# All low parts behind a norm on VectorE, gate rows split in one piece and placed later, retention's output in two parts

## The reference

```python
def rms_norm(x, w):
    y = xf * lax.rsqrt(jnp.mean(xf * xf, axis=-1, keepdims=True) + EPS)
    return (y * w)
# second block
mod = silu(c) @ w_ada + b_ada                     # shift, scale, gate for three parts
u = rms_norm_2(x, ffn1_norm_g) * (1 + sc1) + sh1
x = x + 0.5 * g1 * swiglu(u, ffn1_w_in, ffn1_w_out)
u = rms_norm_2(x, mix_norm_g) * (1 + sc2) + sh2
z = u @ w_mix + b_mix                             # q, k, v, o, i, f of the mLSTM, q, k, v, f of the attention
# mLSTM: b = cumsum(log_sigmoid(f)); m_t = b + running maximum of (i - b)
# retention, per head: ret = rms_norm(forward + backward); y_ret = silu(rg) * ret
```

## Time and profile before

| | us |
|---|---|
| median of 3 runs | 2095.94 |
| lowest, highest | 2094.49, 2096.2 |
| the profiled execution | 2094.88 |
| its span, first to last instruction | 2093.1 |

### The profile page before, as it was taken

One profiled execution on the slowest core, in us unless ns is written; L12 is line 12 of the kernel. 1 busy time (PEld: TensorE's weight loads), 2 busy tenths in 40 slices (PEclk: granted clock), 3 DMA queues, 4 the chain that ended last, 5 costly groups with the idle time before them and its releaser, 6 DMA issues.

```text
span 2093.1 us, 27478 instructions
## 1 busy us (share of the span) xinstructions
PE 2030.0 (97%) x9476; PEld 1594.0 (76%) x9476; DVE 860.5 (41%) x1237; ACT 773.1 (37%) x1176; POOL 771.0 (37%) x310
## 2 busy tenths in 40 slices
PE   7899999999999999999979999999999999999999
PEld 5677677888888788888857776677788887888887
DVE  5566574342232543442284555444311264222200
ACT  5334343322222322322245555555522243223211
POOL 2222243444443444444323322222244434444443
PEclk9999999999999999999989999999999999999999
DMA  4111134553322455552212221111233222323322
GB/s 147 51 51 41 51 108 164 199 186 95 105 95 81 160 185 196 190 180 97 85 51 61 70 70 51 51 53 57 61 91 100 90 90 80 100 90 100 101 94 95
DMA packets 56641, 210.72 MB, mean 101 GB/s; under 512 B 6288, under 2 KB 7056, under 8 KB 56592
## 3 DMA queue, kind: packets, MB, share of 16 engines
q1 hardware_dynamic: 56592, 210.08, 31.1%
HBM read 207.96 MB, written 2.10 MB: 100 GB/s over the span
## 4 chain that ended last, share of the span: by engine, by line
PE 71%; issue 22%; POOL 5%; ACT 1%; DVE 1%; POOLq 0%; ACTq 0%; DVEq 0%
PE bank L431 62%; POOL wlo L376 4%; PE bank L465 1%; PE bank L714 1%; PE bank L768 1%; PE bank L783 1%; PE bank L794 1%; PE bank L803 1%; POOL xl L387 0%; POOL wlo L381 0%; PE bank L487 0%; PE bank L775 0%; PE bank L772 0%; ACT fraw L1242 0%; DVE sqn L1397 0%
## 5 line engine op out<-in xcount | busy, mean ns | idle before, releaser
L376 POOL TENSOR_TENSOR wlo<-raw,whi 128x1024 fp32r<-128x1024 f32 (+1 forms) x290 | 739.2, 2549 | 1262.5 <-ACT whi L872 1262.5
L431 PE MATMUL bank<-xh,whi 128*128 128x512 f32 x1688 | 685.6, 406 | 39.0 <-DVE xl L1388 13.0
L431 PE MATMUL bank<-xh,wlo 128*128 128x512 f32 x1688 | 662.6, 393 | 0.0
L431 PE MATMUL bank<-xl,whi 128*128 128x512 f32 x1688 | 662.6, 393 | 0.0
L872 ACT ACTIVATE whi<-raw 128x1024 fp32r<-128x1024 f32 (+1 forms) x298 | 330.2, 1108 | 630.1 <-PE bank L431 616.2
L431 PEld LDWEIGHTS bank<-xh,whi 128*128 128x128 f32 x1688 | 319.8, 189 | 120.9 <-issue 33.0
L431 PEld LDWEIGHTS bank<-xl,whi 128*128 128x128 f32 x1688 | 320.3, 190 | 69.8 <-issue 7.7
L431 PEld LDWEIGHTS bank<-xh,wlo 128*128 128x128 f32 x1688 | 319.8, 189 | 68.9
L431 PE MATMUL bank<-acth,whi 128*128 128x512 f32 x528 | 209.0, 396 | 0.5 <-POOL wlo L376 0.5
L431 PE MATMUL bank<-acth,wlo 128*128 128x512 f32 x528 | 208.8, 396 | 0.0
L431 PE MATMUL bank<-actl,whi 128*128 128x512 f32 x528 | 208.8, 395 | 0.0
(11 more groups left out here) (314 smaller groups left out, 2050.3 us busy)
## 6 DMA issues: line engine op xcount, KB each, us to landing
raw<-w_dram SPq DMA_DIRECT2D x250, 512.0 KB, 3.6
adaw<-ada_dram SPq DMA_DIRECT2D x72, 512.0 KB, 4.3
raw<-wd_dram SPq DMA_DIRECT2D x48, 704.0 KB, 4.0
h<-x_dram SPq DMA_DIRECT2D x4, 512.0 KB, 7.4
out_dram<-h SPq DMA_DIRECT2D x8, 256.0 KB, 3.7
rel<-rel_dram SPq DMA_DIRECT2D x1, 513.0 KB, 8.0
crow<-c_dram SPq DMA_DIRECT2D x1, 512.0 KB, 3.4
gates_raw<-gates_dram SPq DMA_DIRECT2D x1, 384.0 KB, 8.5
```

What stands on the lines that cost most here:

```text
L376: nc.gpsimd.tensor_tensor(wlo[:, s, 0:width], raw[:, s, 0:width], whi[:, s, 0:width].bitcast(F32), ALU.subtract).then_inc(sem("w_lo"), 1)
L431: mm = nc.tensor.matmul(proj[b][:], w[:, s, W], v[:, k, :], start=first and j == 0 and a == 0, stop=last and j == len(chunks) - 1 and a == ...
```

## The change

Five edits. (1) Behind a norm VectorE makes all eight low parts, and the low parts of the weight slabs 3 and 4 (for norm 3 only slab 3; POOL makes slab 4); POOL waits. ScalarE makes the high part of every chunk with one instruction; for norm 3 its first split stands ahead of chunk 2, not 0. (2) The rows `mrow` and `frow` go into one tile `mf` of 36 partitions (rows 0 to 3 and 32 to 35), which is cleared by a memset, and are split together; ScalarE places all six copies inside head 0, behind its two value tiles, and head 0 is written out ahead of the loop. (3) `ret_out` becomes `ret_gated` (two passes) and `ret_out` (two passes), both moved to block 1 of the next step: the first ahead of `ret_tile(t, 0)`, the second behind the maxima. (4) Ahead of step 0, VectorE ropes the last tile before it evacuates v's tile and scales the second probabilities; TensorE does the first half of retention's first slab ahead of the transposes of v. (5) In the feed-forwards, the split of the slab after next stands ahead of the second silu, and the silu of c, which was the first work of ff0, stands behind the first silu.

```diff
@@ pool
-            def norm_lows(r):
-                n = SLAB[FIRST[r]] + 2
-                norm_low(r, 1)
-                low(n, 0)
-                norm_low(r, 3)
-                low(n + 1, 1)
+            def after_norm(r):
+                n = SLAB[FIRST[r]]
+                if r == 3:
+                    pool.wait_ge(sem("w_lo"), primed(n + 3))
+                    pool.wait_ge(sem("w_hi"), n + 4)
+                    nc.gpsimd.tensor_tensor(wlo[:, 1, 0:WC], raw[:, 1, 0:WC], whi[:, 1, 0:WC].bitcast(F32),
+                                            ALU.subtract).then_inc(sem("w_lo"), 1)
+                else:
+                    pool.wait_ge(sem("w_lo"), primed(n + 4))
@@ tensor: mixing_step, b == 0, and ahead of step 0
-                        wide("ret", t, 4, 0, part=(0, 4))
                         if t > 0:
+                            wide("ret", t, 4, 0, part=(0, 4))
                             ret_sum(t - 1)
...
+            wide("ret", 0, 4, 0, part=(0, 4))
             pe.wait_ge(sem("evac1"), primed(N_ATT // 2))
             transpose_values(vraw, bank[4], "vT")
@@ scalar: norm
-                    if c in POOL_LOW:
-                        nc.scalar.activation(tmp[c % 3], tmp[c % 3], ACT.Identity, bias=sh).then_inc(sem("x_shifted"), 1)
-                        act.wait_ge(sem("x_shifted"), (r - 2) * len(POOL_LOW) + POOL_LOW.index(c) + 1)
-                        nc.scalar.activation(xh[:, c, :], tmp[c % 3], ACT.Copy).then_inc(sem("x_hi"), 1)
-                    else:
-                        nc.scalar.activation(xh[:, c, :], tmp[c % 3], ACT.Identity, bias=sh).then_inc(sem("x_hi"), 1)
+                    nc.scalar.activation(xh[:, c, :], tmp[c % 3], ACT.Identity, bias=sh).then_inc(sem("x_hi"), 1)
@@ scalar: ff_first
+                if run == 0:
+                    act.wait_ge(sem("c_in"), 16)
+                    nc.scalar.activation(crow[:], crow[:], ACT.Silu).then_inc(sem("c_silu"), 1)
                 act.wait_ge(sem("ff_first"), run + 1)
                 nc.scalar.activation(chunk(acth, 0), aprod[:, 0, :], ACT.Copy).then_inc(sem("act_hi"), 1)
                 matmuls(n + 3)
+                split(0, 4, n + 2, 2, WC)
                 nc.scalar.activation(gsil[:, 1, :], proj[0][:], ACT.Silu).then_inc(sem("evac0"), 1)
-                for k in range(2, 4):
-                    split(0, 4, n + 2, k, WC)
+                split(0, 4, n + 2, 3, WC)
@@ scalar: norm 3, mlstm_head
-            norm(3, shift=3, splits={0: 0})
+            norm(3, shift=3, splits={2: 0})
...
+                if first:
+                    act.wait_ge(sem("rows_clear"), 3)
+                    act.wait_ge(sem("row_split"), primed(3))
+                    place_rows(msM, 0)
+                    place_rows(msm, 32)
                 act.preload_act_table(ACT.Silu)
...
-            place_rows(0, msM, slice(0, MH), "m_rows")
-            place_rows(1, msm, slice(0, MH), "m_rows")
-            with act.Fori(0, MH - 1) as hd:
-                mlstm_head(hd)
+            mlstm_head(0, first=True)
+            with act.Fori(0, MH - 2) as i:
+                mlstm_head(i + 1)
@@ vector: norm
+                def weight_low(s):
+                    n = SLAB[FIRST[r]] + 2 + s
+                    dve.wait_ge(sem("w_lo"), primed(n))
+                    dve.wait_ge(sem("w_hi"), n + 1)
+                    V.tensor_tensor(wlo[:, s, 0:WC], raw[:, s, 0:WC], whi[:, s, 0:WC].bitcast(F32),
+                                    ALU.subtract).then_inc(sem("w_lo"), 1)
                 for c in range(3):
                     scaled(c)
-                low(0)
-                scaled(3)
-                scaled(4)
-                low(2)
-                scaled(5)
-                low(4)
-                if beside:
-                    beside()
-                scaled(6)
-                low(5)
-                scaled(7)
-                low(6)
-                low(7)
+                for c in range(KC):
+                    low(c)
+                    if c == 0 and r != 3:
+                        weight_low(0)
+                    if c == 3 and r == 3:
+                        beside()
+                    if c == 5 and r == 3:
+                        weight_low(0)
+                    if c + 3 < KC:
+                        scaled(c + 3)
+                if r != 3:
+                    weight_low(1)
@@ vector: mixing_step
                     if b == 1:
+                        if tail:
+                            ret_gated(t - 1)
                         ret_tile(t, 0)
...
                     if b == 0:
                         ret_decay_logs(t)
-                        if tail:
-                            ret_out(t - 1)
+                    if b == 1 and tail:
+                        ret_out(t - 1)
@@ vector: ahead of step 0
+                normed_rope(p, qall[:, p - 1, :] if p else kf[:])
+                att_scaled(p + 1)
                 if p == QT - 1:
-                    att_scaled(p + 1)
                     win_scale(0, 1)
-                normed_rope(p, qall[:, p - 1, :] if p else kf[:])
-                if p < QT - 1:
-                    att_scaled(p + 1)
@@ vector: rows
-            split_rows(0, H4, mrow)
-            V.tensor_tensor(frow, cs[H4, :], mrow, ALU.add).then_inc(sem("frow"), 1)
+            V.tensor_tensor(mf[F4, :], cs[H4, :], mf[H4, :], ALU.add).then_inc(sem("frow"), 1)
+            dve.wait_ge(sem("frow"), 1)
+            R36 = slice(0, 32 + MH)
+            rest = [mf[R36, :], zt[R36, :], zg[R36, :]]
+            for j in range(3):
+                V.tensor_copy(gsp[R36, j, :], rest[j]).then_inc(sem("row_split"), 1)
+                if j < 2:
+                    dve.wait_ge(sem("row_split"), primed(j + 1))
+                    V.tensor_tensor(rest[j + 1], rest[j], gsp[R36, j, :], ALU.subtract).then_inc(sem("row_rest"), 1)
+                    dve.wait_ge(sem("row_rest"), j + 1)
             for g in range(MH):
                 V.tensor_scalar(sel[:, g, :], ones[0:96, :], c1("sel", g, rows=slice(0, 96)), None,
                                 ALU.mult).then_inc(sem("sel_ready"), 1)
-            dve.wait_ge(sem("frow"), 1)
-            dve.wait_ge(sem("m_rows"), 3)
-            split_rows(1, H4, frow)
```

More of the change, by code:

```diff
@@ L260, in build @@
         NORM = (1, 2, 4)
-        POOL_LOW = (1, 3)
-        def lows_done(r, k):
-            if k in POOL_LOW:
-                return "x_lo1", primed((r - 1) * len(POOL_LOW) + POOL_LOW.index(k) + 1)
-            mine = [c for c in range(KC) if c not in POOL_LOW]
-            return "x_lo0", primed((r - 1) * len(mine) + mine.index(k) + 1)
         def chunk_free(r, c):
@@ L423, in slab @@
                     k = chunks[j]
-                    if ready and ready[0] == "x_lo":
-                        name, count = lows_done(ready[1], k)
-                        pe.wait_ge(sem(name), count)
-                    elif ready:
+                    if ready:
                         pe.wait_ge(sem(ready[0]), primed(ready[1] + k + 1))
@@ L678, in ff_slab @@
                 uses = (TILE[f"ff{run}"] + s) // 2 - (1 if s < 4 else 0)
-                slab(i * 4 + n, s % 2, s % 2, i * 2 + uses, xh, xl, range(KC), ready=("x_lo", NORM[run]) if s == 2 else None)
+                slab(i * 4 + n, s % 2, s % 2, i * 2 + uses, xh, xl, range(KC), ready=("x_lo", KC * (NORM[run] - 1)) if s == 2 else None)
             def ff_tiles(run):
@@ L750, in mlstm_head @@
                 wide("mlstm", hd, 6, 7, part=(6, KC))
-            slab(SLAB["mlstm"] + 1, 1, 1, (TILE["mlstm"] + 1) // 2, xh, xl, range(KC), ready=("x_lo", 3))
+            slab(SLAB["mlstm"] + 1, 1, 1, (TILE["mlstm"] + 1) // 2, xh, xl, range(KC), ready=("x_lo", KC * 2))
             with pe.Fori(0, MH) as hd:
@@ L1148, in _, with place_rows @@
             nc.scalar.activation(zt[0:48, :], zt[0:48, :], ACT.Ln, bias=ones[0:48, 0:1]).then_inc(sem("g_ln"), 1)
-            def place_rows(which, dst, rows, done):
-                act.wait_ge(sem("row_split"), primed(3 * which + 3))
+            def place_rows(dst, at):
                 for j in range(3):
-                    n = rows.stop - rows.start
-                    nc.scalar.activation(dst[32 * j:32 * j + n, :], gsp[rows, j, :], ACT.Copy).then_inc(sem(done), 1)
+                    nc.scalar.activation(dst[32 * j:32 * j + MH, :], gsp[at:at + MH, j, :], ACT.Copy).then_inc(sem("m_rows"), 1)
             def conv_tile(hd, j, i, s):
@@ L1171, in mlstm_weight, with mlstm_head @@
                 nc.scalar.activation(Dm[:, b % 2, 0:P], nMd[:, b * P:(b + 1) * P], ACT.Exp, bias=a).then_inc(sem("m_D"), 1)
-            def mlstm_head(hd, more=True):
+            def mlstm_head(hd, more=True, first=False):
                 n = SLAB["mlstm"]
@@ L1638, in _ @@
             mixing_step(AH // 2 - 1, more=False)
+            ret_gated(AH // 2 - 1)
             ret_out(AH // 2 - 1)
@@ L1806, in _ @@
             V.memset(zrow[:], 0.0).then_inc(sem("zeros"), 1)
+            V.memset(mf[:], 0.0)
```

(10 more changed lines are left out.)

36 lines of the change are left out of this document (13 added, 23 removed).

## The result

The changed kernel takes 2057.2 us (median of 4 runs, 2056.5 to 2057.5), the kernel before, measured beside it, 2095.5 (4 runs, 2094.5 to 2096.2). The ratio is 0.9817, with a 95% interval from 0.980 to 0.9834: 38.3 us faster. The forecast was 2061 with a range from 2052 to 2076. The profiled execution has a span of 2054.7 against 2093.1, so 38.4 us are to be found, and the mean granted TensorE clock is 0.999 against 0.991.

A forecast was written before the change was run, and what follows sets the result against it. TensorE was taken as the bound, with gains only where it stands still. Terms of 35.3 us off the profiled 2094.9 gave 2059.6, plus 1.1 for the median 2060.7, forecast as 2061 us; range 2052 to 2076.

The forecast's parts named there:

- What bounds the kernel: Whole kernel: TensorE is the bound, time comes only from where it stands still, and long waits also bring the low clock.
- Part 1: Norms: VectorE's low parts no longer meet POOL passes; gains 4.6 us in the first, 3.9 second, 3.7 fourth.
- (a): Rival: shorter waits and low clock remain in norms, head's chain meets POOL; gain 22.5, 2073 us; 0.24 together with (b).
- Part 2: Third norm and first mLSTM head: ScalarE no longer waits early for gate rows; gain 10.2 us, bounds 4.2 and 14.8.
- the give-back of 4.6: First mLSTM head: of 14.8 us that could go, 4.6 come back in waits of 1 to 2 us.
- Part 3: Last query tile before step 0: earlier rope, 12 earlier matmuls, no low clock; gain 8.3 us, bounds 3.5 and 9.
- Part 4: Retention's output in three steps: scalings come first, removing TensorE's three waits; gain 4.6 us, bounds 3 and 5.
- (b): Rival: in the norms VectorE's weight low is as slow as POOL's and becomes the bound; 2072 us; 0.24 together with (a).
- (d): Rival: the change moves waits only, each engine's next task being as late as the one removed; 2096 us; chance 0.03.
- (c): Rival: short waits keep TensorE at 1.2 GHz in the six reworked places; gain used up, up to 2106 us; chance 0.04.
- (e): Rival: table-set changes cost more where ScalarE's queue is full, in the head; term 2.6 less, 2064 us; chance 0.04.
- (f): Rival: better than summed, no give-back in the head and none in Part 3; 2054 us; chance 0.08.

The follow-up runs named there:

- experiment 2: The changed kernel, but POOL instead of VectorE makes the two weight lows behind norms 1, 2 and 4: 2064.0 us.
- experiment 4: The changed kernel, but VectorE splits the gate rows in two pieces again, with ScalarE's six copies still at their late place: 2060.8 us.
- experiment 5: The changed kernel with VectorE's old order ahead of retention's first step (evacuation and second scaling before the last rope), TensorE's 12 early matmuls kept: 2064.6 us.
- experiment 6: The changed kernel with TensorE's 12 matmuls of retention's first slab put back behind the start of step 0, VectorE's new order kept: 2064.5 us.
- experiment 1: The changed kernel with the low parts, weight lows and VectorE's order as before in all four norms, POOL making its share again: 2069.1 us.
- experiment 3: The changed kernel with the gate rows still split in one piece, but ScalarE's six copies placed ahead of the first mLSTM head as before: 2065.0 us.
- experiment 9: The changed kernel with another ScalarE order in head 0: v's copies between the silus, what the first scores need ahead of the output gate's tile: 2053.9 us.
- experiment 10: The same kernel as experiment 9, measured again beside the changed kernel: 2054.0 us.
- experiment 8: The changed kernel with retention's output again in one piece of four passes ahead of the two scalings: 2064.3 us.
- experiment 7: The changed kernel with ScalarE's old order behind a norm: silu of c ahead of the first gate tile, both splits behind the second silu: 2059.7 us.
- experiment 11: The kernel of experiment 9 with the second convolution tile and its split also ahead of the gates' two exponentials: 2052.0 us.

## Why the prediction was right

The mechanisms and their places held, and each part came out slightly better than summed; the differences add up to 3.1 us (38.4 - 35.3, 0.2 of it ahead of all parts), most of the 3.8 between forecast and result.

- **What bounds the kernel.** That time comes from where TensorE stands still, and from the low clock behind it, held: the gains lie at the six reworked places, and the stretches between them are as long as before.
- **Part 1.** The pair of VectorE and POOL was read rightly (experiment 2 shows it alone), the weight low of 1.2 was 1.22, and the chain was 14.0 for 14.5. The gain is 0.7 over the sum, 0.5 of it from the chain and 0.3 from what follows it. Two things were read less well. The order of split and silu, which I put at 0.6 in norm 1 and at nothing of its own, is 0.5 in each of three norms, and the silu of c adds about 1.7, only beside slow low parts. And for the clock, which fell to 0.57 in norm 1, there is no term of its own: it is inside the 328.14 from which I subtracted, so the sum isn't wrong by it, but which part of the gain it is I had looked at only in rival (a).
- **Part 2.** 10.2 forecast, 10.45 measured, and the give-back of 4.6 in waits of 1 to 2 us is there: 1.58, 1.96 and 2.10. I had named the copies of v; the weighted scores I had not. The one piece counts by its 3 us of VectorE's chain (experiment 4), and by the clock besides.
- **Part 3.** 8.3 forecast, 9.1 measured, just over my high bound of 9. Its three gains of 2.4, 2.8 and 3.6 are 3.2, 3.1 and 2.8 by experiments 5 and 6 (if the clock costs the same in each), a little too much on the clock and too little on the two moves; the 0.5 that I let come back at the second scaling is there as a wait of 0.46.
- **Part 4.** 4.6 forecast, 5.3 measured, over my bound of 5: the restart of TensorE, 0.2 for each wait removed, was left out.
- **Rivals.** (a) named the right danger: the low clock comes back in each of experiments 1 to 6, but in the kernel after it doesn't fall at any reworked place. That is partly luck in head 0, where the same wait of 1.96 did bring it in experiments 5 and 6, for 1.7 us. (b) fell with the 1.22, and (d), that waits only move on, with experiment 1. (c) fell with the mean clock of 0.999. (e), the dearer change of table set that the Trainium skill gives (ScalarE: Activation LUTs, What ACT_TABLE_LOAD costs), isn't seen: in the kernel after the second load of head 0 runs from 1066.98 to 1068.26, 0.02 behind the silu ahead of it, and the next instruction starts at 1068.28. (f) was 3 us beyond the result; its own terms (4.6 in the head and 0.5 in part 3 on top of 35.3) give 2055.6 and not the 2054 that I wrote. Experiments 9 and 10, which take most of the give-back away, are at 2054 with every part a little better than summed.

**Still open.** Where the clock fell in the two long runs of experiment 8, and what decides at a wait near 2 us whether it falls, wasn't tried.

## What to carry to other kernels

Where VectorE and GpSimd both work in a short, urgent stretch, look for passes of twice their usual length; giving all of it to VectorE can be faster although VectorE then has more to do. Two edits that shorten the same wait don't add up: one may be worth nothing beside the other (the silu of c), or each nearly everything (the two halves of the rope), so undo each alone before it is called useless or essential. When a long wait on a hand-ordered engine is removed, read the order behind it anew: the next gain, 3 us here, lay in copies that had been harmless while TensorE waited anyway. Before a difference of 1 to 3 us between two kernels is given a cause, compare their granted clock in the stretches that neither edit touches.

## What was not expected of the hardware

**The clock doesn't follow from one wait's length.** In the traces here TensorE's granted clock was at the 1.2 GHz level after single waits of 8.25, 4.86, 3.40 and 2.41 us, after 2.06 and 0.89 close together, and after 0.98, 0.59 and 1.84 in norm 1; it stayed at 1.00 after 1.58. Near 2 us, the same code with the same waits did both, at three places. In norm 2 TensorE stood 0.60 and 2.02 in the kernel before, and the clock was 0.60 from 692 to 696; in experiment 1 it stood 0.59 and 2.01, and the clock stayed at 1.00. In head 0 the wait of 1.96 for v's copies left it at 1.00 in the kernel after; in experiment 5 the same stretch, 6 us from the same wait on, is this:

```profile
1077.00:1083.00 6.00, 4.68 (x6) 1.79 (x7) 2.93 (x6) 4.81 (x12) 2.02 (x2) 0.57 0.29 89
```

The third place is a wait of 2.00 in the attention behind the mLSTM, where even the same kernel did both. Stretch from 1224 to 1240 of experiment 9 and of experiment 10, whose spans are 2050.9 and 2052.6:

```profile
1224.00:1240.00 16.00, 13.76 (x61) 8.86 (x59) 9.14 (x17) 10.15 (x20) 4.30 (x3) 1.00 0.20 66
```
```profile
1224.00:1240.00 16.00, 13.84 (x50) 8.74 (x49) 9.13 (x17) 8.46 (x16) 4.03 (x2) 0.89 0.22 66
```

This is 0.11 of 16 us, about 1.7 us, which is the difference between the two spans: a part of the scatter between runs is this, and a forecast to 2 us can't be checked on one run. The traces of experiments 3, 5 and 7 have it at this place too, the other traces don't.

**Small passes meet POOL too, and some with one tensor as input.** A scan on 4 partitions, both inputs in SBUF, took 3.30 beside a POOL pass in the kernel after and 1.21 alone in experiment 3, a cast of 36 partitions 2.50 in experiment 11 for 0.42, and the scaling of probabilities, one tensor and a column, 1.69 at 65.01 of the kernel after for 0.35 at 61.30.
